# A new memory order and a new cell ring for the weights of a four-layer block in split fp32

## What is computed

```python
def hybrid_layer(x, ...):
    h = rms_norm(x, attn_norm_w)
    proj = h @ w_in
    mixed = jnp.concatenate([retention_mixer(...), dsa_mixer(...), dilated_mixer(...)], axis=-1)
    x = x + mixed @ w_out
    h = rms_norm(x, mlp_norm_w)
    return x + jnp.square(jax.nn.relu(h @ w_up)) @ w_down      # w_up 1024x4096, w_down 4096x1024

def swiglu(h, w_gate, w_up, w_down):                           # FFN of the two second layers
    return (jax.nn.silu(h @ w_gate) * (h @ w_up)) @ w_down
```

## Time and profile before

| | us |
|---|---|
| three runs | 2408.21, 2407.44, 2405.17 |
| median | 2407.44 |
| the profiled execution | 2407.12 |
| its span in the profile | 2405.3 |
| TensorE busy | 2356.6 (98%) |
| VectorE, ScalarE, GpSimd busy | 1291.3, 1044.4, 1209.9 |
| mean granted clock of TensorE | 0.996 |

### The profile page before, as it was taken

One profiled execution on the slowest core, in us unless ns is written; L12 is line 12 of the kernel. 1 busy time (PEld: TensorE's weight loads), 2 busy tenths in 40 slices (PEclk: granted clock), 3 DMA queues, 4 the chain that ended last, 5 costly groups with the idle time before them and its releaser, 6 DMA issues. The chain is left out here.

```text
span 2405.3 us, 32546 instructions
## 1 busy us (share of the span) xinstructions
PE 2356.6 (98%) x12840; PEld 1931.1 (80%) x12840; DVE 1291.3 (54%) x2210; ACT 1044.4 (43%) x1654; POOL 1209.9 (50%) x915
## 2 busy tenths in 40 slices
PE   8999999999999999999999999999999999999997
PEld 6777688989877767888987769788889779788887
DVE  4687586565447866766555455322225768322224
ACT  5445564444343456543445455322224485322223
POOL 4435277777343253877773453554454334454442
PEclk9999999999999999999999999999999999999999
DMA  5213123333222221232332212322332312332331
GB/s 164 80 62 106 36 92 102 111 100 98 79 88 88 61 89 53 91 120 88 113 116 77 77 36 71 105 90 85 106 105 88 105 53 89 105 96 80 105 105 53
DMA packets 153975, 214.58 MB, mean 89 GB/s; under 512 B 7776, under 2 KB 94944, under 8 KB 153568
## 3 DMA queue, kind: packets, MB, share of 16 engines
q1 hardware_dynamic: 153824, 212.51, 27.2%
HBM read 208.30 MB, written 2.10 MB: 87 GB/s over the span
## 5 line engine op out<-in xcount | busy, mean ns | idle before, releaser
L410 POOL TENSOR_TENSOR w_lo<-raw,w_hi 128x512 fp32r<-128x512 f32 (+2 forms) x600 | 769.6, 1317 | 1007.2 <-ACT w_hi L349 999.5
L448 PE MATMUL ps<-h_hi,w_hi 128*128 128x512 f32 (+1 forms) x1248 | 509.2, 408 | 10.9 <-POOL w_lo L410 10.6
L448 PE MATMUL ps<-h_hi,w_lo 128*128 128x512 f32 (+1 forms) x1248 | 489.5, 392 | 0.0
L448 PE MATMUL ps<-h_lo,w_hi 128*128 128x512 f32 (+1 forms) x1248 | 489.0, 392 | 0.0
L349 ACT ACTIVATE w_hi<-raw 128x2048 fp32r<-128x2048 f32 (+2 forms) x145 | 247.5, 1726 | 236.1 <-PE ps L448 98.8
L448 PE MATMUL ps<-hid_hi,w_hi 128*128 128x512 f32 x736 | 292.6, 397 | 4.7 <-DVE hid_lo L1114 2.7
L448 PEld LDWEIGHTS ps<-h_hi,w_hi 128*128 128x128 f32 (+1 forms) x1248 | 234.7, 188 | 74.5 <-issue 17.9
L448 PE MATMUL ps<-hid_hi,w_lo 128*128 128x512 f32 x736 | 287.9, 391 | 0.0
L448 PE MATMUL ps<-hid_lo,w_hi 128*128 128x512 f32 x736 | 287.5, 391 | 0.0
L448 PEld LDWEIGHTS ps<-h_lo,w_hi 128*128 128x128 f32 (+1 forms) x1248 | 234.4, 188 | 53.0 <-issue 5.7
L448 PEld LDWEIGHTS ps<-h_hi,w_lo 128*128 128x128 f32 (+1 forms) x1248 | 233.9, 187 | 53.2 <-issue 0.4
(11 more groups left out here) (380 smaller groups left out, 4960.2 us busy)
## 6 DMA issues: line engine op xcount, KB each, us to landing
raw<-in_w_down SPq DMA_DIRECT2D x32, 1024.0 KB, 5.0
raw_u<-in_w_up SPq DMA_DIRECT2D x28, 1024.0 KB, 5.4
raw<-in_ffn_w_gate SPq DMA_DIRECT2D x44, 512.0 KB, 3.9
raw<-in_ffn_w_up SPq DMA_DIRECT2D x44, 512.0 KB, 4.9
raw<-in_w_in SPq DMA_DIRECT2D x20, 1024.0 KB, 5.1
raw<-in_ffn_w_down SPq DMA_DIRECT2D x20, 1024.0 KB, 5.0
raw<-in_w_out SPq DMA_DIRECT2D x8, 1024.0 KB, 5.3
raw<-in_ev_w_in SPq DMA_DIRECT2D x8, 1024.0 KB, 5.3
```

The costliest lines, as they stand in the source:

```text
L410: pool.tensor_tensor(slot.lo(k)[:, 0:slot.width], raw[r][:, k, 0:slot.width], slot.hi(k)[:, 0:slot.width].bitcast(F32), ALU.subtract).then ...
L448: mm = pe.matmul(o, lh, rh, start=first and q == 0, stop=last and q == 2, skip_group_check=True)
```

## The change

- **Memory order.** `dynamic_dma_scratch_size` is set to 1024 bytes and the first tensor starts at 1152 instead of 16512. All that TensorE reads as operands lies low: h from 1152, hid from 33920, w0 and w1 from 66688 to 99456, tables, two work buffers, and a region from 113536 to 182784. Then come x (182784), raw0 and raw1 (199168), vectors and small tensors.
- **Buffers.** w2 lies at 113536, w3 at 129920, w4 at 150496 (and the second layers' accumulator with it), t_hi and t_lo at 113536 and 129920, the "t" cells in the same place.
- **Cells.** Down projections take w0 and w1 in turn, four cells each. Units take a ring of nine "more" cells of their own: eight from the end of the region downward (178688 down to 150016) and one at 225056/227104. Unit n of a group's second slot takes the cell that unit n-2 of its first slot had.
- **First group** (j = 1): `middle(1, 1)` is moved into the loop of the relus of group 0, behind the second low part. `ends(1)` has a wait for the four low parts of the hidden rows.
- **Later groups** (j = 2 to 7): on VectorE and ScalarE the sums and high parts of the second slot stand in another order.

```diff
-        top = [16512]
+        top, end = [1152], [229368]
...
-        for i, off in ((2, region + 16384), (3, region + 32768), (4, region), (5, t_off["h_hi"])):
+        for i, off in ((2, region), (3, region + 16384), (4, acc_at), (5, t_off["h_hi"])):
...
-        for i in range(5):
-            more_cell("more", i, region + 32768 + 4096 * i, region + 32768 + 4096 * i + 2048)
-        more_cell("more", 5, t_off["pT_more"], t_off["stat"])
+        for i in range(8):
+            more_cell("more", i, region_end - 4096 * (i + 1), region_end - 4096 * i - 2048)
+        more_cell("more", 8, t_off["pT_more"], t_off["stat"])
...
-        turn_of_cells = [(b, k) for b in range(2) for k in range(KT)] + [("more", i) for i in range(6)]
+        u_cells = [("more", i) for i in range(9)]
...
-                    slot.cells = [turn_of_cells[(turn + k) % len(turn_of_cells)] for k in range(slot.rows)]
-                    turn += slot.rows
+                    if slot.quarters:
+                        slot.cells = [u_cells[(turn + k) % len(u_cells)] for k in range(slot.rows)]
+                        turn += slot.rows
+                    else:
+                        slot.cells = [(downs % 2, k) for k in range(slot.rows)]
+                        downs += 1
...
                     if j >= 2:
+                        units_hi(act, ua + 1, 2, 3)
+                        p1_copy(j, 0)
                         units_hi(act, ua + 1, 3, 7)
-                        p1_copy(j, 0)
                     rows_hi(act, ua + 2, 0, 4)
                     rows_hi(act, ua + 3, 0, 3)
                     if j >= 2:
...
-                        units_hi(act, ua + 5, 0, 3)
+                        units_hi(act, ua + 5, 0, 2)
...
                     if n >= 1:
                         low(n - 1)
+                    if n == 2:
+                        middle(1, 1)
                 low(3)
                 for j in range(1, CH1):
                     ua = u_slot(j)
                     if j >= 2:
-                        units_sum(dve, ua + 1, 2, 4)
                         for m in range(4):
                             add_out(pl.down[j - 2][1], m, 4 + m)
+                        units_sum(dve, ua + 1, 1, 3)
                         middle(j, 0)
-                    middle(j, 1)
+                        units_sum(dve, ua + 1, 3, 4)
+                        middle(j, 1)
...
-                        units_sum(dve, ua + 5, 0, 2)
+                        units_sum(dve, ua + 5, 0, 1)
...
-    nc = bacc.Bacc("TRN2", target_bir_lowering=False, num_devices=1)
+    nc = bacc.Bacc("TRN2", target_bir_lowering=False, num_devices=1, dynamic_dma_scratch_size=1024)
```

More of the change, by code:

```diff
@@ L37 @@
 HALF = 4
+REGION = 69248
 UNITS = 7
@@ L121, in place @@
                 top[0] += -(-size // 32) * 32
-                assert top[0] <= 229368, (name, top[0])
+                assert top[0] <= end[0], (name, top[0])
             t = nc.alloc_sbuf_tensor_at(name, shape, dt, offset=off)
@@ L128, in two @@
             return t[:].rearrange("p (b t) -> p b t", b=2)
-        x = place("x", [P, DB, S])
         h_hi, h_lo = place("h_hi", [P, DB, S], F32R), place("h_lo", [P, DB, S], F32R)
         hid_hi, hid_lo = place("hid_hi", [P, DB, S], F32R), place("hid_lo", [P, DB, S], F32R)
-        raw = [place(f"raw{i}", [P, KT, 512]) for i in range(RING)]
         w_hi = [place(f"w_hi{i}", [P, KT, 512], F32R) for i in range(RING)]
@@ L136, in build @@
         tab = place("tab", [P, T_SHARED])
+        sq_both = place("sq_both", [P, 2, S])
+        tmp_both = place("tmp_both", [P, 2, S])
+        region, region_end = top[0], top[0] + REGION
+        top[0] = region_end
+        x = place("x", [P, DB, S])
+        raw = [place(f"raw{i}", [P, KT, 512]) for i in range(RING)]
         vec = place("vec", [P, V_ALL])
@@ L140, in build @@
         wf_hi, wf_lo = place("wf_hi", [P, DB, FOX_H], F32R), place("wf_lo", [P, DB, FOX_H], F32R)
-        sq_both = place("sq_both", [P, 2, S])
         sq = [sq_both[:, i, :] for i in range(2)]
         rstd, rs2 = place("rstd", [P, S]), place("rs2", [P, S])
-        tmp_both = place("tmp_both", [P, 2, S])
         tmp = [tmp_both[:, i, :] for i in range(2)]
@@ L156, in build @@
         eps_c, one, spare = (singles[:, i:i + 1] for i in range(3))
-        region = top[0]
-        for i, off in ((2, region + 16384), (3, region + 32768), (4, region), (5, t_off["h_hi"])):
+        end[0] = region_end
+        acc_at = region + 32768 + 4192
+        for i, off in ((2, region), (3, region + 16384), (4, acc_at), (5, t_off["h_hi"])):
             w_hi.append(place(f"w_hi{i}", [P, KT, 512], F32R, where=off))
@@ L1947, in ends @@
                     sg["relu_ready"].by(relu(u_q[0], u_q[0], 1))
+                    if j == 1:
+                        dve.wait_ge(*at("hid_lo_done", HALF))
                     dve.wait_ge(sems["unit_used"], b.unit0 + 5)
@@ L2022, in second_layer @@
             top[0] = region
-            acc = place(f"acc{layer}", [P, DB, S])
+            acc = place(f"acc{layer}", [P, DB, S], where=acc_at)
             macc = place(f"macc{layer}", [P, DB, S], where=t_off["h_lo"])
@@ L2060, in second_layer @@
                 place("xp_end", [P, 6 * (3 + S) - 4 * S])
+                assert top[0] <= acc_at
                 xp = place("xp", [P, 6, 3 + S], where=t_off["gt"] + 4 * 4 * S)
```

5 lines of the change are left out of this document (3 added, 2 removed).

## The result

| | before | after |
|---|---|---|
| median of four runs, us | 2407.82 (2405.17 to 2410.53) | 2474.07 (2473.26 to 2475.99) |
| span of the profiled execution | 2405.3 | 2471.7 |
| TensorE busy | 2356.6 | 2367.4 |
| mean granted clock | 0.996 | 0.985 |

The changed kernel takes 1.0276 times as long (95% interval 1.0258 to 1.0294): 66 us slower. The forecast was 2475.

A forecast was written before the change was run, and what follows sets the result against it. TensorE, busy 2356.6 of 2405.3 us, was taken to bound the kernel. Terms: 2407.1 - 10.9 (Part 1) - 0.5 (Part 2) + 59.4 (Part 3) + 20.4 (The clock) = 2475.5, stated as 2475 us; range 2449 to 2489.

The forecast's parts named there:

- Part 3: Later groups (j = 2 to 7, 12 in all): the new order makes TensorE wait for ScalarE's second copy, +59.4 us.
- The chain fourth sum, GpSimd's unit 2, load, rows, copy: Each later group: fourth sum behind first `middle`, GpSimd's unit 2 5.5 us later, copy ends +20.5; new stall 4.9 us.
- the group of 1012.01: Later group starting at 1012.01 in the trace before, slower load: stall of 6.0 us, of which 0.5 are there already.
- The clock: Behind each new stall in the 12 later groups: lower clock level costs 1.7 us a group, +20.4 us.
- Rival (b): Later groups: two stretches at the lower clock for each stall, 2475 + 12 x 1.7 = 2495 us; 8%.
- The step from two stalls of 2.2 us to "longer ones all do": Later groups: both 2.2 us stalls were followed by the lower clock, so each 4.9 us one is too, 1.7 us each.
- Part 1: Swiglu layers and down projections: 2016 matmuls of 512 columns moved to low addresses gain 5.4 ns each, -10.9 us.
- the quarter groups: Their 256-column matmuls in new cells: taken as 0, ends a gain of 1.6 us or a loss of 2.3 us.
- The rule of the Trainium skill: On weight addresses: TensorE never waits for anyone, so the memory order would give 0 and the sum 10.9 us more.
- Part 2: First group of each first layer: stall at unit 5 moves to the down projection, -0.3 us a layer, -0.5 for both.

The follow-up runs named there:

- Experiment 1: Changed kernel with ScalarE's second copy (j = 2 to 7) ahead of all four rows of the second down projection instead of behind three: 2394.99 us, 0.9946 of before.
- experiment 2: Changed kernel with the earlier ring of 14 cells shared by units and down rows, all orders as changed: 2478.35 us.
- experiment 5: Kernel before with 2j small idle activations on ScalarE ahead of the second copy of quarter groups j = 2 to 7: 2446.70 us.
- experiment 8: Bare-matmul probe ahead of the Experiment 1 kernel, nine low stationary places at 32-byte steps modulo 256: 512 columns 226.7 ns at offsets 0 and 256, 229.0 to 234.1 between.
- experiment 9: Kernel before with the region of w2, w3, w4, the 'more' and 't' cells starting 32 bytes higher, nothing else: 2396.18 us, 0.9956.
- experiment 3: Kernel before with the changed memory order alone, a ring of 14 cells and every engine order as before: 2397.78 us, 0.9961.
- experiment 4: Kernel before with the first group's edit alone (second additions behind the second low part, wait in ends): 2409.27 us over 10 runs, 1.0006.
- experiment 7: Matmul probe in the kernel's pattern, 12 stationary places, ahead of the Experiment 1 kernel: 512 columns 226.7 ns at the first three, 232.2 to 233.4 from 138240 on.

## Why the prediction was right, and where it was not

**Part 3, the order in the later groups: right in its mechanism and its sizes.** The chain fourth sum, GpSimd's unit 2, load, rows, copy came out within 0.2 us at every step. The waits are 57.8 us against 59.9; the group of 1012.01, for which I had 6.0 us because of its slower load in the earlier trace rows, has 4.8 (its load lands sooner now), and another (at 1145) has 5.2. Experiment 1 shows that it is the copy, experiment 2 that it is the order.

**The clock: right in size for this kernel, thin in its ground.** 81.7 us of the groups less 57.3 us of waits and 0.8 us of pitch (from experiment 1) is 23.6 us, 2.0 us a group; the term was 1.7. Rival (b), two stretches behind each stall, is half there (seven of twelve), but all seven begin inside the stall, and the two stretches cost 1.9 to 2.9 us and not 3.4. The step from two stalls of 2.2 us to "longer ones all do" came out right, but experiment 5 shows that 2.2 us was no boundary, so the ground was thinner than the result.

**Part 1, the memory order: right in size, wrong in mechanism.** The term was -10.9 us; the swiglu stretches and the ten down pairs alone gave -11.6. The failing step is "what differs is where the weights lie. [...] So I read an address effect", taken as one of height, with a supposed step between 147000 and 171000. In the trace of before height and the start modulo 256 bytes go together: all weights below 147584 were congruent with the moving tiles, all above 171000 were 32 bytes off. One trace couldn't tell them apart, and I didn't look at the starts' low bits. Experiments 8 and 9 do. The slow down pairs of experiment 3 fit in as well: its cells (150016 to 172544) start 128 past the moving tiles, 232 ns in the kernel and 232.5 ns in experiment 8. That the term came out right in size is because the new order happened to put w0 to w3 congruent with the moving tiles; low places with another offset would have gained next to nothing (table of experiment 8). For the quarter groups, which I put at 0, it means less than +0.1 us each: they left w0 and w1 (congruent, 120 ns) and cells 32 short of it (117 ns) for cells 128 off (119 ns).

The rule of the Trainium skill that the forecast weighed ("SBUF — State Buffer", section "SBUF: two separate sides") says that TensorE waits for no other engine at its ports. No run here speaks against that: in experiment 8 the pitch is 226.7 ns or 229.0 to 234.1 ns with every other engine idle. What fails is the step from it to "an address should not matter": the cost comes from the places of TensorE's own two operands.

**Part 2, the first group: right.** The waits are where I put them, GpSimd's rows 1.2 us later in experiment 4 (1.4 forecast). With this edit alone the trace has 0.6 us less in the two first groups and the time is the same within 0.15%; I had -0.5 us, and the 0.7 us that the next group of the first layer then pays, through the same copy, was missing from the sum.

## What to carry to other kernels

When an order is changed, follow what each engine does next to the transfers it lets go, and from there to whatever stands behind the instruction that waits for them: a small copy in a queue behind a load cost 79 us here, and one line put it ahead. A list of waits names who signalled last (here GpSimd, with a later row), not who was late; an edit that moves the suspect alone settles it. And before a memory layout is redone, the starts of the two matmul operands are worth a look: 32 bytes gave as much as the whole new memory order.

## What the runs showed of the hardware

- Fp32r matmuls of 512 columns follow at 226.7 ns when stationary and moving operand start congruent modulo 256 bytes and at 229.0 to 234.1 ns otherwise; 192 bytes is the mildest offset. With 256 columns the congruent case is among the slowest (119.9 ns, others 117.3 to 119.8). It shows with all other engines idle. Why, no run shows.
- The lower clock level came behind all 28 stalls of TensorE of 3.6 us and more in experiments 2 and 5 and the changed kernel, behind one of 2.07 us and, in all 13 traces, behind one of 2.85 us, and not behind others of 2.20, 2.64, 2.93 and 3.08 us. In three first groups of experiments 7 and 8 it came behind several waits of 0.7 to 1.2 us close together, with no longer one.
